# Order of work inside the input map, and the first loads and waits of the RWKV scan

## The reference, cut to what matters

```python
u = h @ w_in                                    # 1024 -> 4480 columns
rkv = short_conv(u[..., :OFF_WD], conv_rkv)     # r, k, v
w_log = -softplus(-(w0 + tanh(wd) @ w_up)) - 0.5
decay = exp(-exp(w_log))
a = sigmoid(a0 + ad @ a_up)
kk = heads(k * k_k)
kk = kk / max(sqrt(sum(kk * kk)), 1e-12)        # the keys' division
k_dir = k * (1 + (a - 1) * k_a)

def step(S, inp):                               # per head, 64 x 64 state
    sa = S kk_t
    S = S * w_t - sa (kk_t * a_t)^T + v_t k_t^T
    return S, S r_t
o = scan forward + scan backward
```

## Time and profile before

| | before |
|---|---|
| median of three runs | 2978.11 us (2973.72 to 2978.93) |
| the profiled execution | 2980.43 us |
| its span | 2978.6 us |
| PE busy | 2812.2 us (94%) |
| DVE busy | 1541.9 us (52%) |
| ACT busy | 805.3 us (27%) |
| POOL busy | 468.7 us (16%) |
| mean DMA rate over the span | 87 GB/s |
| input map | about 936 to 1443 us of the span |
| scan | about 1443 to 1770 us |

### The profile page before, as it was taken

How to read it: one execution, slowest core, us unless ns; L and a number is a source line. 1 busy time by engine, 2 the same in 40 slices (tenths; PEclk the granted TensorE clock), 3 DMA queues, 4 the chain that set the end, 5 groups by cost and what they waited for, 6 DMA issues and landing times. The chain is left out here.

```text
span 2978.6 us, 53460 instructions
## 1 busy us (share of the span) xinstructions
PE 2812.2 (94%) x21936; PEld 2680.6 (90%) x21936; DVE 1541.9 (52%) x2777; ACT 805.3 (27%) x1409; POOL 468.7 (16%) x561
## 2 busy tenths in 40 slices
PE   7999999999998999999689977899899999999998
PEld 4999999999997988899578865899799999999997
DVE  4456665666536355632477758455633333333335
ACT  4211111111115233444155545221511111111111
POOL 4101001110005001222233324122500000000001
PEclk9999999999999999999799999999999999999999
DMA  6122222222202423444655423312111111111112
GB/s 270 57 71 85 71 84 85 85 76 79 65 13 103 144 101 129 142 140 159 176 118 117 100 95 124 121 67 67 36 41 41 40 41 39 41 41 42 42 43 71
DMA packets 187198, 257.67 MB, mean 87 GB/s; under 512 B 99072, under 2 KB 136960, under 8 KB 185376
## 3 DMA queue, kind: packets, MB, share of 16 engines
q1 hardware_dynamic: 173280, 227.86, 23.6%
q0 software_dynamic: 12608, 27.48, 2.9%
q10 hardware_dynamic: 1152, 0.07, 0.0%
HBM read 200.23 MB, written 55.12 MB: 86 GB/s over the span
## 5 line engine op out<-in xcount | busy, mean ns | idle before, releaser
L845 DVE SCALAR_TENSOR_TENSOR x<-bank,gate,x 128x128 f32<-128x128 f32 (+1 forms) x832 | 409.6, 515 | 199.9 <-PE bank L963 199.3
L1014 ACT ACTIVATE act_out_ffn<-bank 128x384 f32<-128x384 f32 x132 | 64.9, 492 | 1267.8 <-PE bank L948 1267.8
L1017 DVE TENSOR_TENSOR g_ffn<-act_out_ffn,bank 128x384 f32<-128x384 f32 x132 | 73.2, 554 | 616.6 <-ACT act_out_ffn L1014 616.6
L948 PE MATMUL bank<-h_hi_ffn,wlo_a_ffn 128*128 128x384 f32 x1056 | 358.8, 340 | 11.3 <-DVE h_lo_ffn L663 4.5
L948 PE MATMUL bank<-h_lo_ffn,whi_a_ffn 128*128 128x384 f32 x1056 | 356.4, 338 | 0.0
L948 PE MATMUL bank<-h_hi_ffn,whi_a_ffn 128*128 128x384 f32 x1056 | 356.2, 337 | 0.0
L948 PE MATMUL bank<-h_hi_ffn,whi_b_ffn 128*128 128x384 f32 x1056 | 354.9, 336 | 0.0
L948 PE MATMUL bank<-h_lo_ffn,whi_b_ffn 128*128 128x384 f32 x1056 | 354.9, 336 | 0.0
L948 PE MATMUL bank<-h_hi_ffn,wlo_b_ffn 128*128 128x384 f32 x1056 | 354.9, 336 | 0.0
L963 PE MATMUL bank<-g_hi_ffn,wlo_d_ffn 128*128 128x384 f32 x1056 | 354.0, 335 | 0.0
L963 PE MATMUL bank<-g_lo_ffn,whi_d_ffn 128*128 128x384 f32 x1056 | 352.8, 334 | 0.0
(11 more groups left out here) (300 smaller groups left out, 4924.9 us busy)
## 6 DMA issues: line engine op xcount, KB each, us to landing
ada_beside_ffn<-in_ada_w POOLq DMA_DIRECT2D x96, 256.0 KB, 3.6
raw_a_ffn<-in_ffn_w SPq DMA_DIRECT2D x44, 512.0 KB, 4.4
raw_b_ffn<-in_ffn_w SPq DMA_DIRECT2D x44, 512.0 KB, 5.0
raw_d_ffn<-in_ffn_w SPq DMA_DIRECT2D x44, 512.0 KB, 3.7
raw_in<-in_w_in SPq DMA_DIRECT2D x35, 512.0 KB, 5.3
mix<-row_out SPq DMA_DIRECT2D x23, 576.0 KB, 3.1
sc_ar<-streams SPq DMA_DIRECT2D x36, 256.0 KB, 3.7
gates<-mix SPq DMA_DIRECT2D x16, 576.0 KB, 5.2
```

Source lines behind the costliest of these rows:

```text
L845: ins = nc.vector.scalar_tensor_tensor(xs, kit.banks[4 + d % 4][:, a:b], kit.gate[:, gate, d, cond:cond + 1], xs, ALU.mult, ALU.add)
L948: mm = nc.tensor.matmul(kit.banks[2 * slot + j][:, 0:CH], w[q][:, par, cols], v[:, k, toks], start=(k == 0 and m == 0), stop=(k == ku - 1 ...
L1014: return self.nc.scalar.activation(out, a, ACT.Silu)
L1017: self.nc.vector.tensor_tensor(g32, act_out, b, ALU.mult).then_inc(g32_ready, 1)
```

## The change

Three edits in the input map and two in the scan:

- ACT: the first two roots of keys 0 stand behind chunk 0 of tile 9 instead of chunk 1.
- ACT: `square` of the next keys stands behind chunk 1 at w 1 instead of chunk 2.
- DVE: `divide` is cut. Its chunks 0 and 1 stay at w 3, chunk 2 moves to w 4, behind that turn's `low`.
- SP: units 1 to 4 are loaded in a row at the head of the scan. Before, units 3 and 4 stood behind the round trips of units 0 and 1.
- ACT waits for `preset` before the first `turn_block` instead of at the head of the scan; DVE waits for it before the first `row` instead of before the first masking. PE's and POOL's own waits for it stay.

```diff
-                    if (p, c) == (W_AT - 1, 1):
+                    if (p, c) == (W_AT - 1, 0):
                         root(0, 0)
                         root(0, 1)
...
                     if w == 1:
                         if c == 0:
                             kept(ct, 1)
-                        if c == 2 and ct + 1 < CT:
+                        if c == 1 and ct + 1 < CT:
                             square(ct + 1)
...
-            def divide(kc):
-                for c in range(NC):
+            def divide(kc, chunks=range(NC)):
+                for c in chunks:
...
                 if w == 3 and ct + 1 < CT:
-                    divide(ct + 1)
+                    divide(ct + 1, (0, 1))
+                if w == 4 and ct + 1 < CT:
+                    divide(ct + 1, (2,))
                 if w == 4:
                     products(ct, 1)
...
         def sync(sp):
+            for k in range(1, 5):
+                load_unit(sp, k)
             for m in slots:
...
-                if m >= 0 or m < -2:
+                if m >= 0:
                     load_unit(sp, m + 5)
...
-                if -2 <= m < 0:
-
-                    load_unit(sp, m + 5)
...
         def scalar(act):
-            act.wait_ge(S["preset"], 7)
...
+                if m + 2 == 0:
+                    act.wait_ge(S["preset"], 7)
                 if live(m + 2):
                     turn_block(m + 2)
...
         def vector(dve):
             dve.wait_ge(S["masks_in"], 16)
-            dve.wait_ge(S["preset"], 7)
...
                 if s == 6:
+                    if k == 0:
+                        dve.wait_ge(S["preset"], 7)
                     dve.wait_ge(n_in[k % 2], 16 * (k // 2 + 1))
```

## The result

The changed kernel took 2956.22 us (median of four runs, 2955.01 to 2958.13) against 2978.17 of the kernel before in the same job: a ratio of 0.9926, interval 0.9912 to 0.9939. 2959.0 us was forecast. The profiled execution took 2958.13 us over a span of 2956.4, against 2980.43 and 2978.6 before. Measured again beside other kernels, the change came to 0.9934 (0.9920 to 0.9949).

A forecast was written before the change was run, and what follows sets the result against it. TensorE, busy 94% of the span, bounds the kernel, so only its idle time can be won. Input map -12.5, presets -1.7 and loads -4.8 sum to -19.0 us: 2959 us on the median's scale, range 2951 to 2969.

The forecast's parts named there:

- the clock's share: Input map: slow TensorE clock behind the first root's wait loses 0.7 and 0.9 us; nothing taken behind the remainder.
- Roots of keys 0: Input map: PE's 2.47 us wait for the first root goes, with the slow clock behind it; -4.1 us, bound -2.5.
- Squares: Input map: PE's three waits for ACT to square the next keys go; -5.0 us, no clock term.
- Remainder: Input map: PE's 6.14 us wait for the weights' remainder falls to 2.7; -3.4 us, clock bounds -1.1 and +1.
- The later rounds: Input map, later rounds: splitting the division wins nothing; without cover, up to 2 us lost in each of two.
- Presets: Scan head: DVE's first masking no longer waits for POOL's last fill; -1.7 us, bounds -4.3 and 0.
- loads in a row: Scan head: PE's 10.40 us wait for unit 3's load goes, DVE is late next; -4.8 us, bounds -10.4 and 0.
- The masking beside POOL's fills: Scan head: DVE's masking does not contend with POOL's fills; if wrong, unit 1's load would hide most of it.
- An empty scan: Rival, scan: small trips and DVE take up what PE no longer waits for, gain nothing; 2965.6 us, chance 0.15.
- the stall taking it back: Rival, input map: the 3.12 us learning rates' wait at 1196.43 takes back 9.1 us; 2968 us, chance 0.10.
- Nothing takes over: Rival, scan: the whole 4.3 and 10.4 us are won; -27.2, 2951 us, chance 0.08.
- The slower rival: Rival, scan: four small transfers behind units 3 and 4's loads take 7 us more each; +15.5, 2994 us, chance 0.05.

The follow-up runs named there:

- the division alone: The kernel before with only the split of the keys' division around the weights' remainder: ratio 0.9982 (0.9972 to 0.9991).
- presets only: The kernel before with only the waits for the presets moved, loads and input map as before: ratio 0.9994 (0.9985 to 1.0003).
- the scan alone: The kernel before with only the scan's two edits, presets' waits and loads in a row: ratio 0.9976 (0.9967 to 0.9984).
- the stores first: The changed kernel with round 0's second four stores ahead of tile 15's row store on SP: 0.9911 (0.9897 to 0.9926) of the kernel before.
- the loads alone: The kernel before with only the load order changed, units 1 to 4 in a row: ratio 0.9987 (0.9978 to 0.9995).

## Why the prediction was right, point by point

On the whole -19.0 us was forecast, and measured were -22.0 by the medians and 0.9926 and 0.9934, 22 and 20 us, by the two ratios. The mechanism was right in every stage; the clock's share was taken too small.

**Roots of keys 0 (-4.1).** PE's wait is gone, and the root ends 0.2 us before PE wants it, where 0.4 was forecast. Counted from the start of the map, the next products behind it (`L1486` at 1078.30 before, `L1489` at 1075.56 now) come 4.5 us earlier, of which 0.2 is the "issue" wait ahead of them.

**Squares (-5.0).** Three waits of 1.7 are gone and nothing has come in their place. The roots and squares together can also be read from two kernels: the changed input map is on average 478.1 us in six profiles (477.2 to 479.5), the one with the division alone 489.1. That is 11.0 for the forecast 9.1; the second number is a single profile, and the idle time alone differs by 7.3 us, as forecast (7.5), the rest is mostly the clock.

**Remainder (-3.4, the clock at nothing).** The wait fell by 3.46 us, to the forecast 2.7. The clock is the term that was mis-sized. Four profiles of the unchanged input map average 493.5 us (491.8 to 494.5), six of the changed one 478.1: -15.4, against -12.5 forecast. PE's waits in them add up to 19.9 and 8.9 us, so 11.0 are idle time, for 10.9 in the forecast. The loss behind slow clock went from 10.1 to 6.4 us, 3.7 for the 1.6 that stood in the sum (all of it behind the root). The larger part of what was left out, 1.3 us, lies behind the remainder, beyond the bound of -1.1; in single profiles anything from 0 to 3.1 us was lost there. 0.7 us of the 15.4 are neither idle time nor clock and stay unexplained. In the pair of profiles of the result another 1.7 us came back behind the learning rates, with their wait unchanged; the average of all profiles has 0.2 there, so that part of the 16.1 us was luck. Since one and the same wait was followed by anything from 0 to 3.1 us of lost clock, the place for this in a forecast is the range, over every wait left in the stage.

**The later rounds.** Nothing was forecast of the split there, and nothing came of it.

**Presets (-1.7) and loads in a row (-4.8).** Together -6.5 was forecast and -7.1 measured, in the profiles of the result; the averages of the heads to `within(4, 0)`, three profiles with the scan as before (53.3 to 54.3 us) and six with both edits (47.2 to 48.0), give -6.3. The steps that had no number of their own were right: the maskings at once behind PE, PE then held by unit 1's load, unit 3's masking held by DVE and no longer by the load. The terms were worked out as if each stood alone, and measured alone they are -1.2 and -2.9 us (to unit 3's masking; -1.7 and -2.0 to `within(4, 0)`), some 4 us in all. That their sum came out right for both together is thus in part luck. The 0.5 us that PE was to win at unit 1's load did not come: `within(1, 0)` starts 10.4 us behind `within(0, 0)` before, 10.0 to 10.6 in the six profiles with both edits and 11.2 with presets only, whose gain has the size of DVE's 1.2 us for `lane_n` alone. The prediction had the link between them, since it counted the 4.5 us head start of the blocks as slack for the small trips, but put that slack into the presets' term only.

**The masking beside POOL's fills.** The rule drawn on (the Trainium skill, SBUF — State Buffer, "Who interferes with whom": VectorE with one SBUF input does not contend with a GpSimd instruction that only writes) holds in this trace: the maskings at 1430.13 take 1.29 us as before, and this fill beside them 1.80, as in the kernel before:

```profile
1430.52 1.80 POOL L1697 MEMSET sc_xy<- 128x2048 f32 x1
```

**The rivals.** An empty scan is refuted by the scan alone at 0.9976; the stall taking it back, by an unchanged 3.05 us, and by the kernel with the stores first, which shows that it hangs on the queue's order. "Nothing takes over" is refuted by PE's 6.33 us for unit 1's load and 1.67 for unit 3's masking. The slower rival was right that the trips grow: by 3.0 us for both with the loads alone, where it wanted 4.6 for each. The Trainium skill (DMA: Bandwidth & Descriptors, "Queues, rings and completion order") has a completion written only after every earlier write of the same DMA engine, across its queues. The trace agrees that loads on SP's queue lengthen trips on POOL's; whether by that rule or because the engines are busy, no run here separates. In the changed kernel the small trips take 3.3 to 4.5 us in a stretch where the DMA engines are busy for nine tenths of the time in nearly every slice:

```profile
DMA  9789999999999999999999999999999999999999
...
n_blocks<-sc_nkr ACTq DMA_DIRECT2D x7, 8.0 KB, 3.3
n_blocks<-sc_nkr POOLq DMA_DIRECT2D x6, 8.0 KB, 3.6
sc_lane_n<-n_blocks POOLq DMA_DIRECT2D x1, 64.0 KB, 4.5
```

The first row has 40 slices from 1434 to 1447 us; the columns of the others are KB each and the median us from issue to landing.

## What to carry to other kernels

A wait of the engine that bounds the kernel costs its own length and, on this chip, an unsteady amount of slow clock behind it: sum the clock's loss behind every wait of the stage, the ones you leave alone too, and put it in the range. Two edits of one pipeline's head should be costed together, each with the other in place: here they gave 1.2 and 2.9 us alone and 7 together. And a stall that ends on a DMA is not always the DMA's: look at what stands ahead of its issue on the queue, which here was worth a further 5 us for one moved block of stores.

## What had not been expected of the hardware

The clock granted to TensorE behind one and the same 2.68 us wait was 0.50 and 0.60 in one profile, 0.73 and 0.77 in the next and 1.00 in a third. The second and third are of the same kernel. In the six profiles of the changed input map it was 1.00 three times and 0.76 over 7 us three times.

Two more units of loads beside them, 2.5 MB, lengthened the 8 KB stores' landing by 1.2 us and the copy behind it by 1.8 in one profile, and a third unit's worth lengthened the `x_blocks` store from 2.4 to 5.7 us: a small transfer in filled queues waited for a part of what was there, not for all of it.
